# One step of a hybrid decoder layer: the key pages of the sample attention multiplied one per attention slot instead of seven in two slots

## The reference

```
z = rmsnorm(x) @ w_in                      # q, k, v of 4 heads; gates gb, gc and hc of a short convolution
prompt:  o = softmax(q1 k1' + bias) v - lam * softmax(q2 k2' + bias) v     (causal, 4 heads)
sample:  the same for one query against 256 cached keys and its own key;
         k_past = cache_k[page_table]      # 2 pages of 128 keys for each of 8 sequences
h = x + [rmsnorm(o), rmsnorm(gb * conv(gc * hc))] @ w_out
y = rmsnorm(h + hier_moe(rmsnorm(h)))      # 32 experts, 2 of them for each token
```

## Time and profile before

| | |
|---|---|
| median of three runs | 1045.1 us (1043.22 to 1049.14) |
| the profiled execution | 1045.84 us, its span 1044.0 us |
| TensorE busy | 933.8 us, 89% |
| VectorE busy | 598.6 us, 57% |
| ScalarE busy | 501.1 us, 48% |
| GpSimd busy | 236.6 us, 23% |
| mean granted clock | 0.953 |

### The profile page before, as it was taken

One profiled execution on the slowest core, in us unless ns is written; L12 is line 12 of the kernel. 1 busy time (PEld: TensorE's weight loads), 2 busy tenths in 40 slices (PEclk: granted clock), 3 DMA queues, 4 the chain that ended last, 5 costly groups with the idle time before them and its releaser, 6 DMA issues. The chain is left out here.

```text
span 1044.0 us, 13878 instructions
## 1 busy us (share of the span) xinstructions
PE 933.8 (89%) x4977; PEld 728.5 (70%) x4977; DVE 598.6 (57%) x1033; ACT 501.1 (48%) x861; POOL 236.6 (23%) x300
## 2 busy tenths in 40 slices
PE   3899999999999999968887999689999999999971
PEld 3799877887788787945576667467777777777620
DVE  4503533353325332657556316789899999888537
ACT  4523344334333344335312212448888888878412
POOL 1102223223233321314223211041110011100065
PEclk9999999999999999988898999779999999999985
DMA  7132221322132111361064442879999999999786
GB/s 232 46 105 75 86 71 57 110 63 66 52 107 86 41 42 62 111 220 50 7 190 161 141 162 91 363 262 391 396 386 398 395 400 392 387 395 380 266 286 220
DMA packets 86763, 202.33 MB, mean 194 GB/s; under 512 B 11839, under 2 KB 53631, under 8 KB 74406
## 3 DMA queue, kind: packets, MB, share of 16 engines
q1 hardware_dynamic: 76206, 168.40, 45.0%
q0 software_dynamic: 5984, 17.18, 4.8%
q10 hardware_dynamic: 4504, 15.85, 4.1%
HBM read 167.00 MB, written 38.41 MB: 197 GB/s over the span
## 5 line engine op out<-in xcount | busy, mean ns | idle before, releaser
L998 PE MATMUL pj<-n_hi,w_hi 128*128 128x350 f32 (+1 forms) x576 | 199.2, 346 | 3.6 <-DVE n_lo L1318 3.6
L998 PE MATMUL pj<-n_lo,w_hi 128*128 128x350 f32 (+1 forms) x576 | 188.6, 327 | 0.0
L998 PE MATMUL pj<-n_hi,w_lo 128*128 128x350 f32 (+1 forms) x576 | 187.7, 326 | 0.0
L1901 DVE TENSOR_TENSOR e_lo<-e_raw,e_hig 128x2048 fp32r<-128x2048 f32 x64 | 145.8, 2280 | 0.0
L998 PEld LDWEIGHTS pj<-n_hi,w_hi 128*128 128x128 f32 x576 | 109.9, 191 | 32.4 <-issue 30.6
L1280 DVE CUSTOM_DVE_ANT_0 sc<-pj,strip 128x512 f32<-128x512 f32 (+5 forms) x120 | 61.0, 544 | 119.5 <-PE pj L1064 78.0
L1897 ACT ACTIVATE e_hig<-e_raw 128x2048 fp32r<-128x2048 f32 x64 | 122.5, 1918 | 4.5 <-DMA e_raw<-in_w_up 4.0
L998 PEld LDWEIGHTS pj<-n_lo,w_hi 128*128 128x128 f32 x576 | 110.2, 191 | 0.6
L998 PEld LDWEIGHTS pj<-n_hi,w_lo 128*128 128x128 f32 x576 | 110.0, 191 | 0.7 <-issue 0.6
L1949 PE MATMUL pj<-e_hig,xT_hi 128*96 128x512 f32 x256 | 105.2, 411 | 0.0
L1949 PE MATMUL pj<-e_hig,xT_lo 128*96 128x512 f32 x256 | 101.8, 398 | 0.0
(11 more groups left out here) (271 smaller groups left out, 1653.5 us busy)
## 6 DMA issues: line engine op xcount, KB each, us to landing
e_raw<-in_w_gate SPq DMA_DIRECT2D x32, 1024.0 KB, 14.6
e_raw<-in_w_up SPq DMA_DIRECT2D x32, 1024.0 KB
e_raw<-in_w_down SPq DMA_DIRECT2D x32, 1024.0 KB, 14.6
w_raw<-in_w_in SPq DMA_DIRECT2D x24, 512.0 KB, 4.0
expert_rows<-yo ACTq DMA_DIRECT2D x32, 384.0 KB, 8.0
expert_rows<-logits SPq DMA_DIRECT2D x22, 384.0 KB, 4.6
wo_raw<-in_w_out SPq DMA_DIRECT2D x8, 512.0 KB, 5.3
k_page<-in_cache_k SPq DMA_DIRECT2D x16, 256.0 KB, 3.6
```

Source lines behind the costliest of these rows:

```text
L998: ins = pe.matmul(pj[g % 2][:, 0:tn], ws[w][:, P * k:P * (k + 1)], x[:, k, t0:t0 + tn], start=(m == 0), stop=(m == 23))
L1901: eng.tensor_tensor(e_lo[r][:, q, :], e_raw[r][:, q, :], e_hi(par, q).bitcast(F32), ALU.subtract).then_inc(s_lo[q], 1)
```

## The change

One line, the list of slots, is changed for pages 0 to 6. Pages 0, 1, 2 were multiplied in slot 29 and pages 3 to 6 in slot 30; now each of the slots 29 to 35 has one. With it the loads of pages 3 to 9 move: before, pages 3 to 5 were loaded in slot 29 and pages 6 to 9 in slot 30; after it, one each in slots 29 to 35. Nothing else differs, and no instruction is added or removed.

```
-        PAGE_SLOT = [29, 29, 29, 30, 30, 30, 30, 36, 36, 37, 37, 38, 38, 39, 39, 40]
+        PAGE_SLOT = [29, 30, 31, 32, 33, 34, 35, 36, 36, 37, 37, 38, 38, 39, 39, 40]
```

## The result

The changed kernel took 1048.17 us in the median of 13 runs, the kernel before 1044.12 us in its 13. The ratio is 1.0037, with a 95% interval of 1.0024 to 1.0051: the change makes the kernel about 3.9 us slower, within the 0.5% that I had set as the border. The forecast was 1046.3 us, with a range of 1040.0 to 1050.5.

A forecast was written before the change was run, and what follows sets the result against it. TensorE, busy 933.8 of 1044.0 us, was taken as the bound. Terms -8.4 (slot 31), +9.6 (slot 32 weights), -1.5 (slot 33, VectorE free earlier), +1.44 (page 5) gave +1.1 us: 1046.3 us, range 1040 to 1050.5.

The forecast's parts named there:

- Slot 31, -8.4 us: TensorE's 6.50 us stall before slot 31's second score piece goes and the clock stays up: 8.4 us earlier.
- Slot 32, the weights, +9.6 us: Output weights 2 to 7 queue in SyncE behind page 6's load, which waits for page 3; ScalarE and TensorE wait: +9.6 us.
- Slot 33, page 4: Page 4's 1.44 us in slot 33 is covered by VectorE's 4.00 us wait for TensorE.
- Slot 34, page 5, +1.44 us: Page 5 in slot 34 is not covered, as VectorE works without a gap and TensorE waits behind it: +1.44 us.
- Slot 35, page 6: Page 6 in slot 35 lies in VectorE's 5.81 us wait for ScalarE; without that it would cost 1.44 us.
- The sum, +1.1 us: Slots 31 to 34 together: +1.1 us, range +0.4 to +2.2, all work behind moving equally; chance 0.65.
- A: Rival: slot 32's weights do not hold it up, slot 31's gain stays; -5.5 us, 1040 us; chance 0.12.
- B: Rival: after slot 32's idle stretch, half clock lasts longer into slot 33; +5 us, 1051.3 us; chance 0.13.
- C: Rival: slot 32's weights land late, weight 3 after 7.9 us; sum +4, 1049.5 us; chance 0.10.

The follow-up runs named there:

- covered, and weights first: The "all covered" kernel with output weights 2 to 7 issued in slot 31 ahead of its pages; 1036.46 us, ratio 0.9908 to the kernel before.
- all covered: The changed kernel with pages 0 to 6 in slots 29, 30, 30, 31, 31, 35, 35; 1033.54 us, ratio 0.9900 to the kernel before.

## Why the prediction was right, point by point

**Slot 31, -8.4 us.** Right: -8.6 in each of the seven traces with one page in slot 29 and one or two in slot 30. The run with two pages moved splits it in stall and clock as the prediction did.

**Slot 32, the weights, +9.6 us.** The mechanism was right and is shown by two runs, of which one changes nothing but the order of issues. The size was off by 0.7 us in the first trace and 1.7 in the second. I took 4.0 us from issue to landing for weight 2; it was 468.50 - 463.28 = 5.2, near the median of the earlier trace rows that I had as the upper bound. Weights, page and queries were issued together, within 1 us. So slot 33 came 0.4 us later than before (first trace) and 1.4 (second), where I had 0.3 us earlier and a range to 0.8 later. The clock is not in that sum: on the scale of before it came back at about 480 us in the first trace and 482.5 in the second, where it was 479 before.

**Slot 33, page 4.** Right: no shift from slot 33 to slot 34 in either trace.

**Slot 34, page 5, +1.44 us.** Right: +1.45 and +1.30 at slot 35, and undone by moving that page alone. The half clock behind it is no cost of the change against before, which has it too, from 503 to 510 us. What I did not foresee is that it can be absent: with page 5 moved, about 1.3 us more than the page was won.

**Slot 35, page 6.** Right, covered: VectorE waits 4.05 us behind it for ScalarE, where it was 5.81.

**The sum, +1.1 us.** Up to slot 36 the two traces show +1.4 and +1.7. That everything behind slot 36 moves by the same amount was the step that failed: the whole difference is 3.9 us by the ratio, 4.1 by the medians, and 4.3 and 3.0 by the traces, all outside the +0.4 to +2.2 of the sum. That the time of 1048.17 us still lies between 1044.5 and 1048.5 is in part luck: I counted from the median of three runs of before, 1045.1, and that of all 13 is 1.0 us lower. The traces place the rest. The first has 1.3 us more between 530 and 566, the second 0.7. TensorE idles there for about 9 us in every version, and the place at which the clock comes back differs: some 3 us after the work begins in both traces of before, some 5 in both of the changed kernel. From 566 to 664 us another 0.7 and 0.4 are added, which I can't place. These are windows of before (second trace), where TensorE's work begins again at 550.71, then of after, where it begins at 552.74:

```profile
552.00:554.00 2.00, 2.00 (x6) 1.56 (x6) 1.97 (x2) 0.00 (x0) 0.88 (x1) 0.56 0.65 262
554.00:556.00 2.00, 2.00 (x10) 1.61 (x10) 1.56 (x3) 0.00 (x0) 0.00 (x0) 1.00 0.00 0
```

```profile
554.00:556.00 2.00, 2.00 (x6) 1.52 (x6) 1.97 (x2) 0.00 (x0) 0.90 (x1) 0.50 0.65 262
556.00:558.00 2.00, 2.00 (x6) 1.54 (x5) 1.58 (x3) 0.00 (x0) 0.00 (x0) 0.50 0.00 0
558.00:560.00 2.00, 2.00 (x10) 1.61 (x8) 0.00 (x0) 0.00 (x0) 0.00 (x0) 0.94 0.00 0
```

The second place is the expert stage. Between 664 and 697 us the changed kernel gains 1.3 us, and between 889 and 955 it gives 2.2 (first) and 1.4 us (second) back. There ScalarE waits longer for expert weights, in the kernel before (second trace) and in the kernel after, from 890 to 962 us:

```profile
ACT e_hig L1897 <- DMA e_raw<-in_w_up: 4.3, 5, 1.5
```

```profile
ACT e_hig L1897 <- DMA e_raw<-in_w_up: 10.9, 7, 2.4
```

That stage moves about 390 GB/s all along. That TensorE's early start is paid back because the loads are no faster is my reading; no run here tests it. Nor does one show why the clock comes back where it does.

**The rivals.** A (the gain stays) did not happen, but it was real behind the one obstacle, and its -5.5 us lie beside -3.5 by the medians for the weights issued first. B (a longer half clock in slot 33) did not happen at the price it asked for: on the scale of before the clock was back at about 480 us in one trace and 482.5 in the other, against 479 before and 489 where B was to decide. This is the window of the second trace, whose distance is 0.3 us:

```profile
482.00:484.00 2.00, 2.00 (x9) 0.96 (x8) 0.68 (x5) 0.00 (x0) 0.00 (x0) 0.95 0.00 0
```

In the first trace TensorE had half clock until about 1.5 us after slot 33 began, in the second about 3.7. In two experiments a whole stretch of slot 33 ran at half clock, after waits of only 3.37 and 2.15 us. The two long idle gaps that B counts before are one in the rows: only the 6.50 us of slot 31 is long, and the clock's second fall, at about 469 us, follows waits of 1.99 us and less. C (late landing) asked for 7.9 us for weight 3; it took about 6.0 in the first trace and 6.4 in the second.

## What to carry to other kernels

When one list serves two engines, cost it on both: moving a small piece of VectorE's work by a few slots also moved a load, and what hurt was not the 1.4 us of the piece but six unrelated loads queued behind its wait. Put a condition that comes late behind the issues that others need, or, better, move the work to where the trace shows its engine idle; moving it from one slot to each of seven is only right for those of the seven that have room. And let a wait removed be followed to the next engine that becomes late, down to the clock: two versions that stood within 0.2 us of each other at slot 33 were 2.3 us apart one slot later.

## What I had not expected of the hardware

The clock made part of the difference between good versions. In the run "covered, and weights first" a wait of 2.15 us in slot 33 was followed by about 6 us at 1.2 GHz (windows from 470 to 476), and the trace was 2.3 us behind "all covered" at slot 34, though it had issued its weights 4.2 us earlier (450.84 + 2.54 against 453.78 + 3.83, each with its distance from before added) and stood beside it at slot 33. Nor do equal waits give an equal clock: behind 1.11 and 1.59 us the scores of slot 35 ran at half clock in three traces and at full clock in three.

And the two traces of the kernel before lay within 0.3 us of each other for 600 us, though they had started 3.8 us apart. That holds for this program only: the two traces of the changed kernel came to differ by 1.0 us at slot 33 and 1.3 us at the end. So a difference of traces is worth reading only once the start is taken off, and a difference near 1 us only once a second trace shows it too.
